# Block one's input projection: the high weights multiply both parts of a row in one 512-column product

## The chip, the cores and the metric

The kernel runs on one core of a Trainium2 chip. The metric is the device time of one execution in microseconds (us). Three executions of the kernel before took 2816.5, 2816.7 and 2818.31 us; the median is 2816.7 us.

## The reference

Two networks of two layers each run one after the other on 256 tokens with 1024 channels, all in float32. The change lies in the first, and in it only in the input projection `h @ w_in`:

```python
for layer in range(DEPTH):                      # DEPTH = 2
    h = _rmsnorm(x, norm1_g[layer])             # x: 256 x 1024
    proj = h @ w_in[layer]                      # 1024 x 3100
    (aq, af, ai, ag, bq, bkc, ..., cq, ck, cv, cf) = jnp.split(proj, split_at, axis=-1)
    o_a = _hgrn2(aq, af, ai, ag, ...)           # gated recurrence, chunks of 64
    o_b = _nsa(bq, bkc, ...)                    # attention over blocks
    o_c = _fox(cq, ck, cv, cf, ...)             # attention with decay
    x = x + concatenate([o_a, o_b, o_c]) @ w_o[layer]
    h2 = _rmsnorm(x, norm2_g[layer])
    x = x + square(relu(h2 @ w_up[layer])) @ w_down[layer]
```

## The kernel before, in words

Nearly all products are made in float32 accuracy out of three passes in the type float32r. A weight tile is split in a high part `w_hi` (ScalarE copies it into float32r, line 776) and a low part `w_lo` (VectorE subtracts, line 800, into the same ring slot). The other operand, a row of 128 channels by 256 tokens, is split likewise into `hn_hi` and `hn_lo`. A product is then low weights times high row (line 839), high weights times high row (line 843) and high weights times low row (line 846), all accumulated in one PSUM bank; the helper is `split_product`.

**The stage in question.** Each layer of the first network begins with the product `in_t`: 18 column tiles of `w_in`, numbered m = 0 to 17 here, each over 8 tiles k of 128 channels. Its result is channel-major: 128 output channels on the partitions, 256 tokens along the free dimension. TensorE runs 24 matmuls of 256 columns for one m, in `block1_pe`. First come 8 of line 839, then 8 pairs of lines 843 and 846; for m = 0 alone the three passes alternate k by k, as the rows of the operand arrive. The results go by turns to PSUM banks 0 and 2, columns 0 to 255. `wait_banks` lets TensorE start m only when the result of m - 2 has been taken out of its bank (semaphore `drained`), and `wait_split` only when `w_lo` of m is there.

**VectorE's queue.** `block1_dve` writes the order by hand. For each m VectorE does, in this order: the pieces of the gated recurrence that are due there (`hg_dve`, lines 1354 to 1427), the low part of the weights of m + 2 (line 800), the scaling of m's result by the row factor `rstd` into `proj` (`input_scaled`, line 1895, which sets `drained`), and, for m = 6 to 13, one scaled row for a later product (line 1885). The recurrence takes its steps by turns of the engines: VectorE writes exponents (lines 1394 and 1398), ScalarE takes their exponential (line 1467), VectorE multiplies (lines 1414 and 1415), TensorE makes 16 small matmuls (line 1329) behind m = 7, 8, 10, 12, 14 and 16, and VectorE takes the scores from PSUM (line 1427). `dve.drain()` makes VectorE wait until what it has issued is written.

**Loads.** A ring of four slots holds the weight tiles. SyncE loads a slot again (line 2946) as soon as the product that used it has ended, ScalarE splits it (line 776), VectorE subtracts (line 800).

**After the stage** comes `in_a`: the first of its products (line 1600, 32 matmuls in the chain's rows) goes to the bank of m = 16 and waits for its `drained`. GpSimd builds blocks from the results 14 and 15 (line 2114).

Of the kernel before, what the change touches and what calls it, by code (L numbers as in the profile page):

```python
# [22 lines left out]
F32R = mybir.dt.float32r  # L23
BF16 = mybir.dt.bfloat16
ALU = mybir.AluOpType
ACT = mybir.ActivationFunctionType
AX_X = mybir.AxisListType.X

P = 128
D = 1024  # L30
KT = D // P
T = 256
# [134 lines left out]
def period(chunks):  # L167

    return next(n for n in range(2, 2 * SLOTS + 1, 2) if n * chunks % SLOTS == 0)
# [399 lines left out]
def kernel_program(nc, streams, consts, params, x_cm, ctx_cm, out_cm, blocks=(1, 2)):  # L569
    with ExitStack() as stack:  # L570
        free = [-(-nc.sbuf_base // 32) * 32]

        def sb(name, shape, dt=F32):

            at = free[0]
            free[0] += -(-4 * int(np.prod(shape[1:])) // 32) * 32
            assert free[0] <= nc.sbuf_usable_end, name
            return nc.alloc_sbuf_tensor_at(name, shape, dt, offset=at)

        def sem(name):  # L580
            return stack.enter_context(nc.semaphore(name))
# [6 lines left out]
        w_lo = [nc.alloc_sbuf_tensor_at(f"w_lo{n}", [P, SLOT_TILES * P], F32R, offset=ring_at + 4 * SLOT_TILES * P * n)  # L588
                for n in range(SLOTS)]
        w_hi = sb("w_hi", [P, SLOTS, SLOT_TILES * P], F32R)  # L590
        res = sb("res", [P, KT, 2 * T])
        hn_hi = sb("hn_hi", [P, KT, 2 * T], F32R)
        hn_lo = sb("hn_lo", [P, KT, 2 * T], F32R)
        hid = sb("hid", [P, FF2 * 2 * T])
        hid_at = free[0] - 4 * FF2 * 2 * T
        work_at = free[0]
# [23 lines left out]
        bank = [stack.enter_context(nc.psum_tensor(f"bank{b}", [P, 512], F32)) for b in range(8)]  # L620
# [36 lines left out]
        proj = proj_b.rearrange("p (m t) -> p m t", t=T)  # L657
# [56 lines left out]
        used = [sem(f"used{s}") for s in range(SLOTS)]  # L714
        drained = [sem(f"drained{p}") for p in range(2)]
        s = Semaphores(sem)
# [37 lines left out]
        def slot_of(lin, g, c):  # L754
            return (lin.chunk + g.at * lin.cpg + c) % SLOTS
# [9 lines left out]
        def split_number(lin, g, j):  # L765

            return lin.split0 + g.at * len(lin.split) + j + g.i * (g.per * len(lin.split))
# [58 lines left out]
        def wait_split(pe, lin, g, c):  # L826
            pe.wait_ge(s.w_lo, split_number(lin, g, lin.split.index(c)) + 1)

        def split_product(pe, lin, g, c, dst, wait_part, x_hi, x_lo, start=True, stop=True, order=None, by_row=False):

            wait_split(pe, lin, g, c)
            slot = slot_of(lin, g, c)
            order = order or range(lin.tiles[c])
            def low_pass(k):
                if g.at == 0:
                    wait_part(0, k)
                pe.matmul(dst, w_lo[slot][:, k * P:(k + 1) * P], x_hi(k), start=(start and k == order[0]), stop=False)  # L839

            def high_passes(k):
                high = w_hi[:, slot, k * P:(k + 1) * P]
                pe.matmul(dst, high, x_hi(k), start=False, stop=False)  # L843
                if g.at == 0:
                    wait_part(1, k)
                return pe.matmul(dst, high, x_lo(k), start=False, stop=(stop and k == order[-1]))  # L846

            if by_row and g.at == 0:
                for k in order:
                    low_pass(k)  # L850
                    mm = high_passes(k)
            else:
                for k in order:
                    low_pass(k)
                for k in order:
                    mm = high_passes(k)
            mm.then_inc(used[slot_of(lin, g, c)], 1)

        def normed_hi(w):
            return lambda k: hn_hi[:, k, 0:w]  # L860

        def normed_lo(w):
            return lambda k: hn_lo[:, k, 0:w]

        def parity(lin, g):
            return (lin.group + g.at) % 2

        def wait_banks(pe, lin, g):

            before = (lin.group + g.at) // 2 + g.i * (g.per // 2)  # L870
            if not (isinstance(before, int) and before == 0):
                pe.wait_ge(drained[parity(lin, g)], before)

        def wait_products(eng, lin, g):

            c = lin.own - 1
            eng.wait_ge(used[slot_of(lin, g, c)], turn_of(lin, g, c) + 1)
# [128 lines left out]
        def streams_before(n):  # L1006
            return sum(norm_width(i) // T for i in range(n))
# [477 lines left out]
        def input_product(pe, lin, g, c, dst, norm, w):  # L1485

            def wait_part(part, k):
                if c == 0:
                    pe.wait_ge((s.norm_hi, s.split_normed)[part], KT * norm + k + 1)

            split_product(pe, lin, g, c, dst, wait_part, normed_hi(w), normed_lo(w))
# [83 lines left out]
        def block1_pe(pe, l):  # L1575
            if l == 0:
                norm_pe(pe, 0)
            lin = PLAN["in_t", l]
            for m in range(lin.n):
                g = Group(m, m, 0, period(1))  # L1580
                wait_banks(pe, lin, g)
                split_product(pe, lin, g, 0, bank[2 * parity(lin, g)][:, 0:T],
                              lambda part, k: pe.wait_ge((s.norm_hi, s.split_normed)[part], KT * 2 * l + k + 1),
                              normed_hi(T), normed_lo(T), by_row=True)
                if m == 0 and l:
                    norm_pe(pe, 2 * l)
                if m == SLOT_DIAG and l == 0:
                    pe.wait_ge(s.consts1, 16)
                hg_pe(pe, l, m)
            lin = PLAN["in_a", l]  # L1590
            for m in range(lin.n):
                g = Group(m, m, 0, period(2))
# [4 lines left out]
                for tt in range(TT):  # L1597
                    q = slice(tt * P, (tt + 1) * P)
                    for k in range(KT):
                        mm = pe.matmul(bank[2 * parity(lin, g)][:, q], sq[:, k, q],  # L1600
                                       ring[slot_of(lin, g, 0)][:, k * P:(k + 1) * P],
                                       start=(k == 0), stop=(k == KT - 1))
                mm.then_inc(used[slot_of(lin, g, 0)], 1)
                compress_pe(pe, l, m, lin, g, 1)
                for u in HEAD_SQUARES[m]:
                    if u == 0:
                        pe.wait_ge(s.hn_sq, l + 1)
                    if u >= 2:
                        pe.wait_ge(s.hn_ln, 5 * l + u - 1)
                    pe.matmul(bank[4 + u % 2][:, :], blk64, sq_b[:, u * 2 * T:(u + 1) * 2 * T],  # L1610
                              start=True, stop=True).then_inc(s.hn_ms, 1)
                if m == 5:
                    pe.wait_ge(s.qkn, l + 1)
                    for u in range(2):
                        pe.matmul(bank[4 + u][:, :], rot, qkn_b[:, (2 + 2 * u) * T:(4 + 2 * u) * T],
                                  start=True, stop=True).then_inc(s.rotated, 1)
# [38 lines left out]
            lin = PLAN["wo", l]  # L1655
            for m in range(lin.n):
                g = Group(m, m, 0, period(1))
# [5 lines left out]
            lin = PLAN["down", l]  # L1663
            for g in turns(pe, lin):
                wait_banks(pe, lin, g)
                for c in range(lin.cpg):
# [3 lines left out]
                                  start=(c == 0), stop=(c == lin.cpg - 1))  # L1670
# [217 lines left out]
        def input_scaled(dve, l, m):  # L1888

            lin = PLAN["in_t", l]  # L1890
            g = Group(m, m, 0, period(1))
            if m == 0:
                dve.wait_ge(s.rstd, streams_before(2 * l) + 1)
            wait_products(dve, lin, g)
            dve.tensor_tensor(proj[:, m, :], bank[2 * parity(lin, g)][:, 0:T], rstd[:, 0:T],
                              ALU.mult).then_inc(drained[parity(lin, g)], 1)

        def square(dve, k, c0, c1):

# [1163 lines left out]
```

## Time and profile before

| | |
|---|---|
| median of three executions | 2816.7 us |
| the profiled execution's own time | 2819.7 us |
| its span in the profile | 2817.5 us |
| TensorE matmuls busy | 2736.7 us (97%), 16508 instructions |
| VectorE busy | 1790.5 us (64%), 3059 instructions |
| ScalarE busy | 1056.1 us (37%) |
| GpSimd busy | 192.0 us (7%) |

The span reaches from the first to the last instruction of the profiled execution; the time of an execution includes a little around it, here 2.2 us. Busy time of an engine is the time covered by its instructions. Matmuls overlap in the pipeline, so the pace of TensorE is read from the distance between starts and not from the duration of one.

### The profile page before, as it was taken

The numbers are of one execution on the slowest core, as the hardware profiler recorded it, in microseconds if no ns is written. First come the engines' busy times: TensorE is split into PE (matmuls) and PEld (weight loads), VectorE is DVE, ScalarE is ACT, GpSimd is POOL, SyncE is SP. The second block draws the span as 40 slices with busy tenths as digits, with TensorE's granted clock in tenths as the row PEclk, the third lists the DMA queues.
The fourth block names the chain that finished last, engine by engine and source line by source line (L and its number), as shares of the span: only waits on it lengthen the run. The fifth ranks groups of instructions, "written<-read, shape, count | busy, mean of one in ns | idle before, by whom it ended". The sixth has DMA issues, their size and how long they took to land.

```text
span 2817.5 us, 45112 instructions
## 1 busy us (share of the span) xinstructions
PE 2736.7 (97%) x16508; PEld 2331.2 (83%) x16508; DVE 1790.5 (64%) x3059; ACT 1056.1 (37%) x1667; POOL 192.0 (7%) x184
## 2 busy tenths in 40 slices
PE   8999999999999999999999999999999999899998
PEld 8669999589988888775777788888788888689998
DVE  8466666566675655597675665655765557757665
ACT  4355443456342221335344322222322213554443
POOL 1000000000000000032213000000000000134000
PEclk9999999999999999999999999999999999999999
DMA  5535554545534443322432244443344433244554
GB/s 202 207 110 193 180 182 159 197 147 184 180 135 149 141 140 132 109 71 70 138 127 67 90 142 149 141 142 127 135 141 147 139 127 125 79 128 158 170 178 157
DMA packets 118649, 401.16 MB, mean 142 GB/s; under 512 B 12928, under 2 KB 20992, under 8 KB 118144
## 3 DMA queue, kind: packets, MB, share of 16 engines
q1 hardware_dynamic: 115408, 392.48, 41.3%
q10 hardware_dynamic: 3120, 7.07, 0.7%
q8 instruction: 76, 1.25, 0.2%
q14 instruction: 45, 0.37, 0.0%
HBM read 398.45 MB, written 1.05 MB: 142 GB/s over the span
## 4 chain that ended last, share of the span: by engine, by line
PE 86%; DVE 5%; issue 4%; DMA 1%; ACT 1%; POOL 1%; DVEq 1%; ACTq 0%; POOLq 0%; SPq 0%
PE bank L839 24%; PE bank L846 24%; PE bank L843 24%; PE bank L1600 2%; DMA ring<-weights 1%; PE bank L2146 1%; PE bank L2505 1%; PE bank L2502 1%; PE bank L2499 1%; DVE work L2267 1%; DVE hn_lo L1072 1%; PE bank L937 1%; POOL w_lo L800 1%; PE bank L1329 1%; PE bank L2175 1%
## 5 line engine op out<-in xcount | busy, mean ns | idle before, releaser
L776 ACT ACTIVATE w_hi<-ring 128x1024 fp32r<-128x1024 f32 (+1 forms) x548 | 572.6, 1046 | 1192.3 <-DMA ring<-weights 1192.2
L800 DVE TENSOR_TENSOR w_lo<-ring,w_hi 128x1024 fp32r<-128x1024 f32 (+1 forms) x538 | 658.7, 1225 | 532.2 <-ACT w_hi L776 528.1
L843 PE MATMUL bank<-hn_hi,w_hi 128*128 128x256 f32 (+1 forms) x2880 | 905.4, 333 | 0.0
L846 PE MATMUL bank<-hn_lo,w_hi 128*128 128x256 f32 (+1 forms) x2880 | 905.1, 333 | 0.0
L843 PEld LDWEIGHTS bank<-hn_hi,w_hi 128*128 128x128 f32 x2880 | 548.5, 190 | 52.2
L846 PEld LDWEIGHTS bank<-hn_lo,w_hi 128*128 128x128 f32 x2880 | 548.5, 190 | 52.2
L839 PE MATMUL bank<-hn_hi,w_lo 128*128 128x256 f32 (+1 forms) x2880 | 577.3, 336 | 11.2 <-DVE w_lo L800 7.7
L839 PEld LDWEIGHTS bank<-hn_hi,w_lo 128*128 128x128 f32 x2880 | 458.4, 190 | 72.5 <-issue 11.1
L843 PE MATMUL bank<-hid_hi,w_hi 128*128 128x512 f32 (+1 forms) x704 | 248.7, 362 | 0.0
L846 PE MATMUL bank<-hid_lo_a,w_hi 128*128 128x512 f32 (+1 forms) x640 | 226.2, 362 | 0.0
L967 DVE SCALAR_TENSOR_TENSOR conds<-ring,con 128x1024 f32<-128x1024 f32 x106 | 130.9, 1235 | 48.3 <-DMA ring<-weights 31.1
L839 PE MATMUL bank<-hid_hi,w_lo 128*128 128x512 f32 (+1 forms) x704 | 156.4, 362 | 0.0
L843 PEld LDWEIGHTS bank<-hid_hi,w_hi 128*128 128x128 f32 x704 | 132.9, 189 | 20.6
L839 PEld LDWEIGHTS bank<-hid_hi,w_lo 128*128 128x128 f32 x704 | 121.9, 189 | 20.6
L846 PEld LDWEIGHTS bank<-hid_lo_a,w_hi 128*128 128x128 f32 x640 | 120.8, 189 | 18.7
L969 DVE SCALAR_TENSOR_TENSOR ring<-ring,con 128x1024 f32<-128x1024 f32 x106 | 131.6, 1241 | 0.0
L843 PE MATMUL bank<-up_hi,w_hi 128*128 128x256 f32 x512 | 125.6, 283 | 0.0
L846 PE MATMUL bank<-up_lo,w_hi 128*128 128x256 f32 x512 | 125.6, 283 | 0.0
L2855 DVE SCALAR_TENSOR_TENSOR hid<-work,par,hid 128x512 f32<-128x512 f32 (+1 forms) x180 | 117.4, 707 | 4.8
L2919 POOL MEMSET work<- 128x1716 f32 x2 | 3.1, 1527 | 1492.0 <-issue 789.3
L843 PEld LDWEIGHTS bank<-up_hi,w_hi 128*128 128x128 f32 x512 | 98.3, 192 | 0.0
L846 PEld LDWEIGHTS bank<-up_lo,w_hi 128*128 128x128 f32 x512 | 98.3, 192 | 0.0
(350 smaller groups left out, 3086.8 us busy)
## 6 DMA issues: line engine op xcount, KB each, us to landing
ring<-weights SPq DMA_DIRECT2D x694, 512.0 KB, 3.4
ring<-weights SPq DMA_DIRECT2D x32, 384.0 KB, 3.1
ring<-weights SPq DMA_DIRECT2D x32, 256.0 KB, 2.9
ring<-weights SPq DMA_DIRECT2D x28, 192.0 KB, 2.4
con<-consts ACTq DMA_DIRECT2D x1, 2063.0 KB, 9.6
con<-consts ACTq DMA_DIRECT2D x1, 1088.0 KB, 5.7
res<-ctx_cm ACTq DMA_DIRECT2D x1, 1024.0 KB, 7.9
con<-params ACTq DMA_DIRECT2D x1, 1024.0 KB, 10.4
```

The source lines that it names most:

```text
L776: act.activation(w_hi[:, slot, 0:w], ring[slot][:, 0:w], ACT.Copy).then_inc(s.w_hi, 1)
L800: eng.tensor_tensor(w_lo[slot][:, 0:w], ring[slot][:, 0:w], w_hi[:, slot, 0:w].bitcast(F32), ALU.subtract).then_inc(s.w_lo, 1)
L839: pe.matmul(dst, w_lo[slot][:, k * P:(k + 1) * P], x_hi(k), start=(start and k == order[0]), stop=False)
L843: pe.matmul(dst, high, x_hi(k), start=False, stop=False)
L846: return pe.matmul(dst, high, x_lo(k), start=False, stop=(stop and k == order[-1]))
L937: mm = pe.matmul(ada_bank(h)[rows, :], cs[:, k, COND_AT - 2 * q:COND_W - 2 * q], ring[slot][:, i * 4 * P:(i + 1) * 4 * P], start=(q == 0 a ...
L967: dve.scalar_tensor_tensor(out=conds[:, :], in0=ring[slot][:, :], scalar=1.0, in1=crow[:, 0:D], op0=ALU.mult, op1=ALU.mult, accum_out=to[: ...
L969: dve.scalar_tensor_tensor(out=ring[slot][:, :], in0=ring[slot][:, :], scalar=1.0, in1=crow[:, D:2 * D], op0=ALU.mult, op1=ALU.mult, accum ...
L1072: last = dve.scalar_tensor_tensor(out=hn_lo[:, k, t], in0=sq[:, k, t], scalar=modulation(l)[:, SHIFT[which], k, c:c + 1], in1=hn_hi[:, k, ...
L1329: mm = pe.matmul(bank[6 + hh][:, c0:c0 + P], keys, queries, start=True, stop=True)
L1600: mm = pe.matmul(bank[2 * parity(lin, g)][:, q], sq[:, k, q], ring[slot_of(lin, g, 0)][:, k * P:(k + 1) * P], start=(k == 0), stop=(k == K ...
L2855: last = dve.scalar_tensor_tensor(out=dst, in0=src, scalar=taps[:, m, k:k + 1], in1=dst, op0=ALU.mult, op1=ALU.add)
```

## The change

The product of the high weights with the high and with the low part of a row becomes one matmul of 512 columns: both parts stand in one tensor, `hn_both`, and the bank's two halves of 256 columns take one result each. The pass of the low weights adds into the first half. VectorE adds the halves with a reduction over the pair, waits for it with a drain, and scales in a second instruction. Both layers are changed (18 results each), and nothing else: other products use `hn_hi` and `hn_lo` as before, at the same addresses. A result takes 8 matmuls of 256 and 8 of 512 columns in place of 24 of 256.

```diff
-        hn_hi = sb("hn_hi", [P, KT, 2 * T], F32R)
-        hn_lo = sb("hn_lo", [P, KT, 2 * T], F32R)
+        hn_both = sb("hn_both", [P, 2, KT, 2 * T], F32R)
+        hn_hi, hn_lo = hn_both[:, 0, :, :], hn_both[:, 1, :, :]
...
+        def joined_product(pe, lin, g, c, wait_part, x_hi, x_both, start=True, stop=True, half=0):
+
+            wait_split(pe, lin, g, c)
+            slot, to = slot_of(lin, g, c), bank[2 * parity(lin, g) + half]
+            rows = lin.tiles[c]
+
+            def low_pass(k):
+                if g.at == 0:
+                    wait_part(0, k)
+                return pe.matmul(to[:, 0:T], w_lo[slot][:, k * P:(k + 1) * P], x_hi(k), start=False, stop=False)
+
+            def high_pass(k):
+                if g.at == 0:
+                    wait_part(1, k)
+                return pe.matmul(to.rearrange("p (u t) -> p u t", u=2), w_hi[:, slot, k * P:(k + 1) * P], x_both(k),
+                                 start=(start and k == 0), stop=(stop and k == rows - 1))
+
+            high_pass(0)
...
+                for k in range(rows):
+                    low_pass(k)
+                for k in range(1, rows):
+                    mm = high_pass(k)
+            mm.then_inc(used[slot], 1)
...
-            dve.tensor_tensor(proj[:, m, :], bank[2 * parity(lin, g)][:, 0:T], rstd[:, 0:T],
-                              ALU.mult).then_inc(drained[parity(lin, g)], 1)
+            dve.tensor_reduce(proj[:, m, :], bank[2 * parity(lin, g)].rearrange("p (u t) -> p t u", u=2), AX_X,
+                              ALU.add)
+            dve.drain()
+            dve.tensor_tensor(proj[:, m, :], proj[:, m, :], rstd[:, 0:T], ALU.mult).then_inc(drained[parity(lin, g)], 1)
```

TensorE's queue at layer 0, m = 8, with the last matmul of m = 7 and the recurrence's 16 small matmuls (one row for 8 of each bank, line 1329 before, 1359 now) ahead of it. Before, where the 8 pairs of lines 843 and 846 follow:

```order
L846 MATMUL bank<-hn_lo,w_hi 128x256
L1329 MATMUL bank<-hid,work 128x128 x8
L839 MATMUL bank<-hn_hi,w_lo_53 128x256 x8
L843 MATMUL bank<-hn_hi,w_hi 128x256
L846 MATMUL bank<-hn_lo,w_hi 128x256
```

And now (line 873 is the matmul of 512 columns, line 868 the pass of the low weights):

```order
L873 MATMUL bank<-hn_both,w_hi 128x512 x7
L1359 MATMUL bank<-hid,work 128x128 x8
L873 MATMUL bank<-hn_both,w_hi 128x512
L868 MATMUL bank<-hn_both,w_lo_53 128x256 x8
L873 MATMUL bank<-hn_both,w_hi 128x512 x7
```

One matmul of the high weights now stands ahead of the low pass, because it opens the whole bank; the other seven stand behind it.

VectorE's queue at layer 0, m = 8 (`hid` holds `proj`, `work` holds `rstd`). Before:

```order
L1394 TENSOR_TENSOR work<-work 128x16x16
L1398 TENSOR_TENSOR work<-work 128x16x16
L1427 COPY_PREDICATED hid<-con_72,bank 128x512 x2
L800 TENSOR_TENSOR w_lo_55<-ring_51,w_hi 128x1024
L1895 TENSOR_TENSOR hid<-bank,work 128x256
L1885 SCALAR_TENSOR_TENSOR work<-res,par_74,work 128x256
```

And now:

```order
L1424 TENSOR_TENSOR work<-work 128x16x16
L1428 TENSOR_TENSOR work<-work 128x16x16
L1457 COPY_PREDICATED hid<-con_71,bank 128x512 x2
L800 TENSOR_TENSOR w_lo_55<-ring_51,w_hi 128x1024
L1925 TENSOR_REDUCE hid<-bank 128x256
L1928 TENSOR_TENSOR hid<-hid,work 128x256
L1915 SCALAR_TENSOR_TENSOR work<-res,par_73,work 128x256
```

No instruction of VectorE changes its place; one is replaced by two.

## Rows read from the trace of the kernel before

**Rows 1.** The page: busy time by engine, chain that ended last by engine.

```profile
PE 2736.7 (97%) x16508; PEld 2331.2 (83%) x16508; DVE 1790.5 (64%) x3059; ACT 1056.1 (37%) x1667; POOL 192.0 (7%) x184
...
PE 86%; DVE 5%; issue 4%; DMA 1%; ACT 1%; POOL 1%; DVEq 1%; ACTq 0%; POOLq 0%; SPq 0%
```

**Rows 2.** Busy time of the engines in the stage, layers 0 and 1.

```profile
core 0: us, PE busy (x) PEld busy (x) DVE busy (x) ACT busy (x) POOL busy (x), PEclk, DMA share, GB/s
...
28.90:74.30 45.40, 45.31 (x409) 43.79 (x410) 41.47 (x73) 18.04 (x20) 6.16 (x8) 1.00 0.46 150
...
415.00:462.50 47.50, 47.50 (x430) 45.98 (x429) 43.14 (x74) 21.07 (x22) 6.18 (x8) 1.00 0.47 156
```

**Rows 3.** Chain of waits (start us, us, what): two passes of 256, two of 512 columns.

```profile
32.12 0.96 PE bank L839 x8
...
35.00 0.96 PE bank L839 x8
...
818.31 1.81 PE bank L839 x8
...
823.75 1.81 PE bank L839 x8
```

**Rows 4.** The same chain where TensorE starts m = 5 of layer 0.

```profile
28.60 0.34 DVE hid L1895
...
28.99 1.21 PE bank L839 x8
```

**Rows 5.** Timeline, VectorE, layer 0 (start us, us, what, [idle before <-releaser]).

```profile
21.88 1.22 DVE L800 TENSOR_TENSOR w_lo<-ring,w_hi 128x1024 fp32r<-128x1024 f32 x1 [2.03 <-ACT w_hi L776]
...
24.45 0.41 DVE L1359 TENSOR_SCALAR work<-work,small 128x256 f32<-128x256 f32 x1 [0.66 <-ACT work L1459]
...
28.52 0.42 DVE L1895 TENSOR_TENSOR hid<-bank,work 128x256 f32<-128x256 f32 x1
28.85 1.22 DVE L800 TENSOR_TENSOR w_lo<-ring,w_hi 128x1024 fp32r<-128x1024 f32 x1
...
50.29 0.42 DVE L1414 TENSOR_TENSOR work<-work 128x256 f32<-128x256 f32 x1 [0.33 <-PE bank L1329]
...
55.60 1.23 DVE L800 TENSOR_TENSOR w_lo<-ring,w_hi 128x1024 fp32r<-128x1024 f32 x1 [0.61 <-ACT w_hi L776]
...
64.37 0.43 DVE L1414 TENSOR_TENSOR work<-work 128x256 f32<-128x256 f32 x1 [0.72 <-PE bank L1329]
...
70.25 0.41 DVE L1895 TENSOR_TENSOR hid<-bank,work 128x256 f32<-128x256 f32 x1
...
81.63 0.42 DVE L1414 TENSOR_TENSOR work<-work 128x256 f32<-128x256 f32 x1 [6.09 <-PE bank L1329]
```

**Rows 6.** Timeline, TensorE: `in_a` starts, layers 0 and 1.

```profile
74.20 1.06 PE L1600 MATMUL bank<-ring,work 128*128 128x128 f32 x8
...
462.53 3.74 PE L1600 MATMUL bank<-ring,work 128*128 128x128 f32 x32
```

**Rows 7.** Timeline, VectorE, layer 1.

```profile
402.35 0.42 DVE L1926 TENSOR_TENSOR work<-bank,work 128x256 f32<-128x256 f32 x1 [2.43 <-PE bank L846]
402.86 0.42 DVE L1929 TENSOR_TENSOR res<-work,res 128x256 f32<-128x256 f32 x1
...
408.03 1.23 DVE L800 TENSOR_TENSOR w_lo<-ring,w_hi 128x1024 fp32r<-128x1024 f32 x1 [0.52 <-ACT w_hi L776]
...
411.85 0.42 DVE L1895 TENSOR_TENSOR hid<-bank,work 128x256 f32<-128x256 f32 x1 [0.84 <-PE bank L846]
...
458.58 0.41 DVE L1895 TENSOR_TENSOR hid<-bank,work 128x256 f32<-128x256 f32 x1
```

**Rows 8.** Groups by form: reductions of VectorE.

```profile
L2184 DVE TENSOR_REDUCE small<-bank 128x1 f32<-128x512 f32 x32 | 22.0, 686 | 8.5 <-PE bank L2146 8.3
...
L1204 DVE TENSOR_REDUCE small<-bank 128x1 f32<-128x256 f32 x40 | 15.1, 419 | 11.3 <-PE bank L1134 10.9
```

More of the change, by code:

```diff
@@ L857, in split_product @@
             mm.then_inc(used[slot_of(lin, g, c)], 1)
+        def joined_product(pe, lin, g, c, wait_part, x_hi, x_both, start=True, stop=True, half=0):
[12 more added lines that the diff above has]
+            high_pass(0)
+            if g.at == 0:
+                low_pass(0)
+                for k in range(1, rows):
+                    low_pass(k)
+                    mm = high_pass(k)
+            else:
+                for k in range(rows):
+                    low_pass(k)
+                for k in range(1, rows):
+                    mm = high_pass(k)
+            mm.then_inc(used[slot], 1)
         def normed_hi(w):
@@ L1581, in block1_pe @@
                 wait_banks(pe, lin, g)
-                split_product(pe, lin, g, 0, bank[2 * parity(lin, g)][:, 0:T],
-                              lambda part, k: pe.wait_ge((s.norm_hi, s.split_normed)[part], KT * 2 * l + k + 1),
-                              normed_hi(T), normed_lo(T), by_row=True)
+                joined_product(pe, lin, g, 0,
+                               lambda part, k: pe.wait_ge((s.norm_hi, s.split_normed)[part], KT * 2 * l + k + 1),
+                               lambda k: hn_hi[:, k, 0:T], lambda k: hn_both[:, :, k, 0:T])
                 if m == 0 and l:
```

## The prediction

> **What bounds the kernel now.** I read the page first. TensorE is busy for 97% of the span and makes 86% of the chain that ended last [rows 1]: fewer TensorE cycles count, if nothing else takes their place. VectorE's 64% is an average over stages. So next I cut out the two stretches in which the changed product runs. There TensorE is busy throughout, but VectorE is busy for 41.47 of 45.40 us in layer 0 and 43.14 of 47.50 us in layer 1, 91% in both, at a TensorE clock of 1.00, its upper level of 2.4 GHz [rows 2]. It has some 4 us to spare per layer, and the change gives it more work there 18 times. Last I looked at who waits for whom. The chain already goes through VectorE once: TensorE starts m = 5 at 28.99, right behind the scaling of m = 3 that ends at 28.94 [rows 4, 5].
>
> **TensorE's part.** Two starts of the 256-column pass lie 35.00 - 32.12 = 2.88 us apart with 24 matmuls between them, 120 ns each; in a 512-column stage it is 823.75 - 818.31 = 5.44 us for 24, 226.7 ns each [rows 3]. One 512-column matmul in place of two of 256 saves 240 - 226.7 = 13.3 ns. There are 8 x 18 x 2 = 288 such pairs, 3.8 us in all, or 0.107 us for each m (2.77 in place of 2.88 us). That is the whole gain, since the array still streams the same columns; 288 weight loads go too, but the gap between starts already contains what they cost. The Trainium skill (TensorE: Matmul & The Clock Gate, "Back-to-back issue gap") gives a fixed 2.5 ns per warm matmul on top of N/2.4; by it the gaps would be 109.2 and 215.8 ns and the whole gain 0.7 us. The rows show about 13 ns above the streaming time at both widths, so I go by them.
>
> No row has a moving operand made of two pieces. Below, that costs nothing; above, I estimate the point at which it would matter. From 50.29 to 64.37 VectorE handles four m's, with 0.61 and 0.72 us idle [rows 5], so two take it (14.08 - 1.33) / 2 = 6.4 us now and 7.9 us after the change. TensorE has two m's and 16 small matmuls to do in that time, now 14.08 / 2 = 7.04 us and then 6.83. Sixteen wide matmuls could each be 65 ns slower before it showed. I cost it at nothing.
>
> **VectorE's part.** One scaling of 0.42 us becomes a reduction, a drain and a scaling. The nearest row for the reduction is one of 512 PSUM elements at 686 ns [rows 8]. A drain between two dependent instructions sets the second 0.51 us behind the first where the first lasts 0.42 (lines 1926 and 1929) [rows 7]: 0.09 us. The second instruction is a 256-element product, 0.42 us like the one removed, and what follows can start 0.33 us behind its start as now (28.52 to 28.85) [rows 5]. So each m adds **a = 0.69 + 0.09 = 0.78 us** to VectorE's queue. The bounds of the reduction: 0.42 us if it went by its 256 outputs, as a reduction of 256 elements does [rows 8], so a = 0.51; twice 0.686 us if the stride of 256 between the two addends halved its rate, so a = 1.46. I take 0.69, the row with the same number of elements read from PSUM. The Trainium skill (VectorE: DVE Perf Modes, the section on the TRN2 errata) has a cycle table, 120 + N from PSUM and 58 + N within SBUF at 0.96 GHz. It would make a 0.66 + 0.09 + 0.33 - 0.39 = 0.68 and the total below 9.0 instead of 11.9 us. The traced 0.42 and 0.69 us are longer than its values, and the sum uses them.
>
> **What reaches the end.** Behind the reduction stand, on VectorE's queue, the scaling that frees the bank for m + 2, the low weights of m + 3 and every piece of the recurrence; TensorE waits for each of them. I follow the queue to the scaling of m = 16, for which `in_a` must wait.
>
> Layer 0. The reductions of m = 0 and 1 are covered, because VectorE idles 2.03 us for ScalarE at 21.88 [rows 5]. Of m = 2's 0.78 us the idle 0.66 before line 1359 covers all but 0.12 [rows 5]. From m = 3 on the queue is nearly full: the idle pieces are 0.33, 0.61 and 0.72 us, 1.66 in all [rows 5]. VectorE now finishes the scaling of m = 16 at 70.66; it would finish 0.12 + 14 x 0.78 - 1.66 = 9.38 us later, at 80.04, and `in_a` would start at 80.09 in place of 74.20 [rows 6]: **+5.9 us**. TensorE's own end gives less: m = 17 needs the bank of m = 15, ready at 68.38 + 0.12 + 13 x 0.78 - 1.66 = 76.98, and ends 2.77 later, at 79.8.
>
> Layer 1. The reductions of m = 0 and 1 are covered by the idle 0.52, 0.19 and 0.84 us ahead of m = 2 (two of them in [rows 7]). From m = 2 on there are 15 reductions up to m = 16, and idle pieces of 0.17, 0.57, 0.33, 0.35 and 0.75 us, 2.17 in all. The scaling of m = 16, now ending at 458.99, would end 11.70 - 2.17 = 9.53 us later, at 468.52, and `in_a` start at 468.57 in place of 462.53: **+6.0 us**.
>
> TensorE's 3.8 us are hidden: it arrives early and waits for VectorE. The sum is +11.9 us. Against the profiled execution's 2819.7 us that is 2831.6; the median of the runs lies 3.0 us lower, so I forecast 2816.7 + 11.9 = **2828.6 us**. Behind the stage I expect no recovery: the ring is only four slots deep, so the weight loads start later by as much, and VectorE idles 6.09 us at its next wait [rows 5], so it no longer matters there. Late next in the stage are the low weights and, once, the recurrence: its matmuls behind m = 8 wait for scores that VectorE takes at about 45.6 in place of 41.7.
>
> **The rivals.**
>
> *The reduction is dearer (0.10).* Its two addends stand 1 KB apart, and no row has such a read. At twice the price each of the 29 uncovered reductions adds another 0.69 us: 19.9 us more, 2848.5 us. For it: it is unmeasured. Against it: element for element, VectorE's PSUM reads of 512 elements all take about 0.69 us in this trace.
>
> *The reduction is cheaper (0.08).* At a = 0.51 the sum falls by 29 x 0.27 = 7.8 us: 2820.8 us, not distinguishable from before.
>
> *VectorE's slack covers it (0.05).* The place is the scaling of m = 16. `in_a` starts on time in layer 0 if 14a is at most 74.20 - 0.05 - 70.66 - 0.12 + 1.66 = 5.03 us, and in layer 1 if 15a is at most 462.53 - 0.05 - 458.99 + 2.17 = 5.66 us: a up to 0.36 us. Then TensorE's gain shows, for 13 m's in layer 0 (the wait at m = 5 eats the first five) and 18 in layer 1: 31 x 0.107 = 3.3 us, 2813.4 us. Against it: even the lower bound of a is 0.51. By the fixed gap of the Trainium skill's page TensorE: Matmul & The Clock Gate this would be 2816.1 us.
>
> *Half is caught up later (0.07).* Behind the stage TensorE also has idle time; if part of it depends on something that does not move, each layer gives back about 3 us: 2822.6 us. Against it: every load and every engine there follows TensorE's own progress.
>
> **How the numbers follow.** My forecast has 0.70. About 0.2%, 5.6 us, is what a measurement of this kernel can tell from no change: faster is below 2811.1, slower above 2822.3. Slower: the forecast, the dear reduction and half of the recovery, 0.70 + 0.10 + 0.04 = 0.84. The same: the cheap reduction, the covered case and the other half, less a small part, 0.14. Faster: 0.02. For the range, a between 0.65 and 0.95 alone gives 2824.8 to 2833.5; I reach down to 2820.5, which takes in the cheap reduction and the recovery, and up to 2840, a reduction half as dear again (10 us more), which leaves out the doubled one.
>
> **What would show it.** In the profile after: reductions of about 0.69 us, 36 of them, and the multiply 0.78 us behind each; 512-column starts 227 ns apart; VectorE without gaps from m = 3 to m = 16; TensorE idle in the stage, with the scaling, the low weights or the recurrence's scores as releaser; `in_a` starting near 80.1; the distance from there to layer 1's stage unchanged. The forecast is wrong if TensorE shows no new idle time there, or if the reduction lasts over 0.95 us.

## The result and the profile after

| | before | after |
|---|---|---|
| median of six executions each | 2816.6 us | 2831.1 us |
| lowest to highest | 2815.68 to 2818.86 | 2827.9 to 2831.58 |
| span of the profiled execution | 2817.5 us | 2829.7 us |
| its own time | 2819.7 us | 2831.5 us |

The ratio is 1.0047, with a 95% interval of 1.0037 to 1.0057: 13.2 us slower, 10.4 to 16.1. The two medians lie 14.5 us apart. The forecast was 2828.6 us, 11.9 us slower. Among the experiments below, three executions (one of e3, two of e10) took between 5354 and 11227 us; they are in no median here.

The page of the kernel after begins with these rows, which answer to [rows 1]:

```profile
PE 2742.1 (97%) x16220; PEld 2320.4 (82%) x16220; DVE 1812.5 (64%) x3095; ACT 1052.9 (37%) x1667; POOL 196.2 (7%) x184
...
PE 84%; DVE 6%; issue 4%; DMA 2%; DVEq 1%; ACT 1%; POOL 1%; ACTq 0%; SPq 0%; POOLq 0%
```

TensorE has 288 matmuls fewer, but busy time on the page says little. The busy time in the stage of the two layers, against [rows 2] (the window and its length, then TensorE, weight loads, VectorE, ScalarE, GpSimd, the granted clock, DMA share, GB/s), tells more; the third row is a short piece that is discussed at the end:

```profile
28.80:79.50 50.70, 46.62 (x305) 38.46 (x305) 48.77 (x82) 16.25 (x19) 7.13 (x8) 0.97 0.40 135
418.90:472.50 53.60, 48.84 (x317) 40.04 (x315) 51.52 (x87) 19.31 (x22) 7.13 (x8) 0.97 0.42 138
46.00:50.50 4.50, 4.50 (x18) 3.90 (x18) 4.17 (x9) 1.06 (x1) 0.00 (x0) 0.62 0.02 4
```

VectorE is now busy for 96% of the stage in both layers (91% before), and TensorE for 92 and 91% (over 99% before). The two have changed roles. TensorE's timeline in layer 0 (start us, duration us, what, idle before and its releaser) shows where it waits:

```profile
28.84 0.50 PE L873 MATMUL bank<-hn_both,w_hi 128*128 128x512 f32 x1 [1.10 <-DVE hid L1928]
...
35.71 0.50 PE L873 MATMUL bank<-hn_both,w_hi 128*128 128x512 f32 x1 [1.02 <-DVE hid L1928]
...
44.68 1.16 PE L1359 MATMUL bank<-work 64*128 64x128 f32 x16 [1.82 <-DVE hid L1457]
...
75.98 0.50 PE L873 MATMUL bank<-hn_both,w_hi 128*128 128x512 f32 x1 [0.61 <-DVE hid L1928]
...
79.48 2.72 PE L1630 MATMUL bank<-ring,work 128*128 128x128 f32 x22 [0.44 <-DVE hid L1928]
```

The releaser is VectorE each time: the scaling (line 1928) or, once, the recurrence's scores (line 1457). `in_a` starts at 79.48 in place of 74.20 [rows 6]. VectorE's timeline, for m = 3 and 4 and at the end of the stage:

```profile
27.60 0.69 DVE L1925 TENSOR_REDUCE hid<-bank 128x256 f32<-128x512 f32 x1
28.36 0.43 DVE L1928 TENSOR_TENSOR hid<-hid,work 128x256 f32<-128x256 f32 x1
28.70 1.22 DVE L800 TENSOR_TENSOR w_lo<-ring,w_hi 128x1024 fp32r<-128x1024 f32 x1
29.84 0.68 DVE L1925 TENSOR_REDUCE hid<-bank 128x256 f32<-128x512 f32 x1
...
50.42 0.69 DVE L1925 TENSOR_REDUCE hid<-bank 128x256 f32<-128x512 f32 x1 [0.26 <-PE bank L873]
...
76.01 0.99 DVE L1424 TENSOR_TENSOR work<-work 128x256 f32<-128x256 f32 x1
76.93 0.94 DVE L1428 TENSOR_TENSOR work<-work 128x256 f32<-128x256 f32 x1
77.80 0.68 DVE L1925 TENSOR_REDUCE hid<-bank 128x256 f32<-128x512 f32 x1
78.55 0.88 DVE L1928 TENSOR_TENSOR hid<-hid,work 128x256 f32<-128x256 f32 x1
```

The reduction takes 0.68 to 0.69 us and the scaling starts 0.76 us behind it. What follows starts 28.70 - 27.60 = 1.10 us behind the reduction, where it started 0.33 us behind the single scaling [rows 5]: a result adds 0.77 us to VectorE's queue. The idle 0.26 us at 50.42 is the only gap that the timeline shows in it from m = 3 to m = 16.

In both layers the comparison below uses three numbers of each profile: the start of `in_a` in layer 0, the length of layer 1's stage (from the first matmul of its norm, 405.03 before, to the start of `in_a`), and the median of the whole. Changes are against the profile of before (74.20 and 57.50 us).

| kernel | `in_a`, layer 0 | stage, layer 1 | sum | median | ratio, 95% interval |
|---|---|---|---|---|---|
| after | +5.28 | +6.06 | +11.3 | 2831.1 | 1.0047 [1.0037, 1.0057] |
| e6, after unaltered | +5.66 | +6.11 | +11.8 | 2833.45 | 1.0055 [1.0041, 1.0069] |
| e1, no reduction | -1.15 | -1.20 | -2.3 | 2816.02 | 0.9997 [0.9988, 1.0006] |
| e2, narrow matmuls | +5.20 | +5.70 | +10.9 | 2828.26 | 1.0048 [1.0035, 1.0061] |
| e3, ScalarE copies half | +3.71 | +3.68 | +7.4 | 2826.98 | 1.0034 [1.0022, 1.0046] |
| e4, reduction alone | +0.59 | -0.33 | +0.3 | 2819.01 | 1.0006 [0.9997, 1.0015] |
| e5, reduction twice | +14.61 | +15.84 | +30.5 | 2848.57 | 1.0113 [1.0098, 1.0129] |
| e7, layer 1 alone | +0.23 | +6.13 | +6.4 | 2823.86 | 1.0027 [1.0017, 1.0036] |
| e8, GpSimd later | +4.08 | +4.84 | +8.9 | 2829.62 | 1.0049 [1.0035, 1.0062] |
| e9, e3 and e8 and an order | +2.41 | +2.53 | +4.9 | 2827.84 | 1.0035 [1.0021, 1.0049] |
| e10, before unaltered | -0.25 | +0.48 | +0.2 | 2818.77 | 1.0003 [0.9993, 1.0013] |

The kernel before, run beside them, had medians of 2816.64 (e1 to e4), 2816.52 (e5 to e8) and 2816.48 us (e9, e10).

### The profile page after: what moved, and what is told of

Same layout as the page of the kernel before. It is cut to its first block, busy times and chain, and to the rows that moved or that the text cites. A ratio compares the mean times of both kernels' runs of the same rounds, so it can differ in the third digit from the quotient of the medians.

```text
span 2829.7 us, 44608 instructions
## 1 busy us (share of the span) xinstructions
PE 2742.1 (97%) x16220; PEld 2320.4 (82%) x16220; DVE 1812.5 (64%) x3095; ACT 1052.9 (37%) x1667; POOL 196.2 (7%) x184
## 4 chain that ended last, share of the span: by engine, by line
PE 84%; DVE 6%; issue 4%; DMA 2%; DVEq 1%; ACT 1%; POOL 1%; ACTq 0%; SPq 0%; POOLq 0%
PE bank L839 23%; PE bank L846 23%; PE bank L843 23%; PE bank L1630 2%; DMA ring<-weights 2%; DVE w_lo L800 1%; PE bank L2178 1%; PE bank L2537 1%; PE bank L2534 1%; PE bank L2531 1%; PE bank L967 1%; POOL w_lo L800 1%; DVEq L1927 1%; PE bank L1539 1%; PE bank L2207 1%
## 5 line engine op out<-in xcount | busy, mean ns | idle before, releaser
L843 PE MATMUL bank<-hn_both,w_hi 128*128 128x256 f32 (+1 forms) x2592 | 834.2, 338 | 0.0
L846 PE MATMUL bank<-hn_both,w_hi 128*128 128x256 f32 (+1 forms) x2592 | 834.0, 338 | 0.0
L839 PE MATMUL bank<-hn_both,w_lo 128*128 128x256 f32 (+1 forms) x2592 | 533.0, 341 | 9.7 <-DVE w_lo L800 8.0
L843 PEld LDWEIGHTS bank<-hn_both,w_hi 128*128 128x128 f32 x2592 | 493.3, 190 | 52.1
L846 PEld LDWEIGHTS bank<-hn_both,w_hi 128*128 128x128 f32 x2592 | 493.2, 190 | 52.0
L839 PEld LDWEIGHTS bank<-hn_both,w_lo 128*128 128x128 f32 x2592 | 420.8, 190 | 68.6 <-issue 10.4
```

## The experiments

The expectations call the theories T1 (VectorE's added time sets the stage and hides what TensorE gains), T2 (the 512-column matmul or TensorE's clock is what got slower) and T3 (joining saves only 2.5 ns a pair).

**e1: the joined product alone.** VectorE works as before, and the second half of the bank is never added.

```diff
-            dve.tensor_reduce(proj[:, m, :], bank[...].rearrange("p (u t) -> p t u", u=2), AX_X, ALU.add)
-            dve.drain()
-            dve.tensor_tensor(proj[:, m, :], proj[:, m, :], rstd[:, 0:T], ALU.mult).then_inc(...)
+            dve.tensor_tensor(proj[:, m, :], bank[2 * parity(lin, g)][:, 0:T], rstd[:, 0:T],
+                              ALU.mult).then_inc(drained[parity(lin, g)], 1)
```

> The changed kernel, in which VectorE does what it did before: one multiply of 256 elements, from the bank's first half (the product of the low part of the row is computed but left out of the sum, in both layers). Theory 1 (the cost is VectorE's added time a per result, 0.77 us, and TensorE's gain is hidden behind it): with a = 0 the gain shows, 31 results x 0.107 us = 3.3 us, so 2813.3 us; in_a of layer 0 starts near 72.8 and of layer 1 about 3 us earlier than before; no wait for line 1928's place of over 2 us. Theory 2 (the 512-column product itself is slower, by its operand in two pieces or by TensorE's lower clock): 2820 us or more, since nothing of it is undone here. Theory 3 (the two weight loads and matmuls saved are worth only about 2.5 ns a pair): 2816.1 us.

Measured: `in_a` starts 1.15 us earlier in layer 0, and layer 1's stage is 1.20 us shorter. The whole slowdown is gone with VectorE's part of it. In layer 0 TensorE waits once, 1.69 us ahead of m = 5 as before, and from there on never again; in layer 1 it never waits. Its clock is 1.00 (windows view of e1, columns as above):

```profile
28.60:73.00 44.40, 44.25 (x304) 37.48 (x305) 41.65 (x73) 18.29 (x20) 6.15 (x8) 1.00 0.46 152
414.40:458.60 44.20, 44.11 (x306) 37.30 (x305) 40.82 (x72) 18.84 (x21) 6.16 (x8) 1.00 0.48 155
```

T2 falls: the wide matmul is no slower. T3's 0.2 to 0.3 us per layer is too little, but my 1.4 and 1.9 us were too much, 2.35 in place of 3.3 us in all. Nor is all of the 2.35 TensorE's gain. m = 5 starts 0.28 us earlier than before (28.71 against 28.99), because the split by ScalarE that VectorE waits for ahead of m = 2 [rows 5] starts 0.29 us earlier (20.50 against 20.79), and that start varies by itself: it is 20.53 in e10, the kernel before once more. From the start of m = 5 to `in_a` it is 44.34 us against 45.21, so 13 results gain 0.87 us there. That and the 1.20 us of layer 1 make some 0.07 us for each result. In the time of an execution even this doesn't show: 0.9997, with 1 in the interval.

**e2: VectorE's part alone, nearly.** Six of the eight wide matmuls of a result are two of 256 columns again, into the same two halves; m = 0 keeps all eight wide.

```diff
-                for k in range(1, rows):
-                    mm = high_pass(k)
+                for k in range(1, rows - 1):
+                    high = w_hi[:, slot, k * P:(k + 1) * P]
+                    pe.matmul(to[:, 0:T], high, x_hi(k), start=False, stop=False)
+                    pe.matmul(to[:, T:2 * T], high, x_both(k)[:, 1, :], start=False, stop=False)
+                mm = high_pass(rows - 1)
```

> VectorE as in the changed kernel (reduction, drain, multiply), TensorE nearly as before: of each result's 8 products of 512 columns, six are split again into two of 256 (the first and the last stay wide, m = 0 keeps all), same sums. Theory 1: TensorE's pace of 2.85 us is still faster than VectorE's, so the time is that of the changed kernel, 2831 us, within 1.5 us; in_a starts at 79.5 in layer 0. Theory 2: back towards 2817 to 2820 us. Theory 3 says the same as theory 1.

Measured: a ratio of 1.0048 against 1.0047, and stages within 0.1 and 0.4 us of those of after. Whether TensorE has its gain or not makes no difference once VectorE adds the halves. This and e1 are the two halves of T1.

**e3: less work for VectorE.** ScalarE copies the upper half out of PSUM; VectorE adds it with an instruction of 256 elements in place of 512.

```diff
+                act.activation(rope_t[:, m % 2 * T:(m % 2 + 1) * T], bank[2 * parity(lin, g)][:, T:2 * T],
+                               ACT.Copy).then_inc(s.upper, 1)
...
-            dve.tensor_reduce(proj[:, m, :], bank[...].rearrange("p (u t) -> p t u", u=2), AX_X, ALU.add)
+            dve.wait_ge(s.upper, lin.n * l + m + 1)
+            dve.tensor_tensor(proj[:, m, :], bank[...][:, 0:T], rope_t[:, m % 2 * T:(m % 2 + 1) * T], ALU.add)
```

> The changed kernel with a cheaper add: ScalarE copies the bank's upper half into SBUF (about 0.4 us, on an engine with 27 us to spare per layer), VectorE adds it to the lower half with a product-sized instruction of 0.42 us instead of the 0.69 us reduction, drain and multiply as now; the sum is the same. Theory 1: a falls from 0.77 to 0.51, 29 x 0.26 = 7.5 us less than the changed kernel: 2823.5 us; up to 2826 if ScalarE's splits, now queued behind its copy, come late. Theory 2: 2831 us.

Measured: 3.71 and 3.68 us in the stages, less than after but more than expected; 2826.98 us in place of 2823.5, and above the 2826 that were allowed for late splits. VectorE's queue in e3 has two new waits for ScalarE's copy, at m = 2 and at m = 16:

```profile
24.61 0.42 DVE L1933 TENSOR_TENSOR hid<-bank,work 128x256 f32<-128x256 f32 x1 [1.69 <-ACT work L1810]
...
74.96 0.94 DVE L1429 TENSOR_TENSOR work<-work 128x256 f32<-128x256 f32 x1
76.94 0.42 DVE L1933 TENSOR_TENSOR hid<-bank,work 128x256 f32<-128x256 f32 x1 [1.04 <-ACT work L1810]
```

ScalarE's own queue explains both. The copy of m = 2 stands behind a split, a table load and three activations of the recurrence; the copy of m = 16 stands behind the exponential that needs VectorE's exponents.

```profile
21.68 1.28 ACT L1488 ACT_TABLE_LOAD   x1
...
24.14 0.37 ACT L1810 ACTIVATE work<-bank 128x256 f32<-128x256 f32 x1
...
75.93 0.63 ACT L1498 ACTIVATE work<-work 128x512 f32<-128x512 f32 x1 [5.48 <-DVE work L1429]
76.47 0.36 ACT L1810 ACTIVATE work<-bank 128x256 f32<-128x256 f32 x1
```

TensorE had finished m = 16 at about 72.8, so the copy could have run in ScalarE's idle 5.48 us; instead VectorE waited for it afterwards, 1.04 us. The first wait makes TensorE wait 1.78 us for the scaling of m = 3, until 30.43, where it went on at 28.84 in after. Layer 1 has the same two waits, 1.76 and 1.04 us (before 416.59 and 468.56). The direction agrees with T1; the expected size left these waits out.

**e4: a smaller a, 0.27 us.** The reduction stays and drain and scaling go, so the row factor is left out of the results.

```diff
             dve.tensor_reduce(proj[:, m, :], bank[...].rearrange("p (u t) -> p t u", u=2), AX_X,
-                              ALU.add)
-            dve.drain()
-            dve.tensor_tensor(proj[:, m, :], proj[:, m, :], rstd[:, 0:T], ALU.mult).then_inc(...)
+                              ALU.add).then_inc(drained[parity(lin, g)], 1)
```

> The changed kernel with the reduction alone: the row factor is left out (drain and multiply gone), so a = 0.69 - 0.42 = 0.27 us per result, below the 0.36 us that VectorE's slack was worked out to cover. Theory 1: TensorE is the bound again, its gain shows, 2813 to 2815 us, and in_a of layer 0 starts between 72.8 and 74. If the slack is really smaller, with the same mechanism, up to 2818. Theory 2: 2825 us or more.

Measured: +0.59 us in layer 0 and -0.33 us in layer 1, where e1 has -1.15 and -1.20; 2819.01 us, which is above the expected 2813 to 2815 and the 2818 allowed beyond it. I had put the point from which the slack covers a at 0.36 us, so 0.27 should have been free. TensorE's timeline of e4 shows why it wasn't:

```profile
29.39 0.50 PE L873 MATMUL bank<-hn_both,w_hi 128*128 128x512 f32 x1 [2.15 <-DVE hid L1925]
...
33.47 2.29 PE L873 MATMUL bank<-hn_both,w_hi 128*128 128x512 f32 x8
...
43.24 1.16 PE L1359 MATMUL bank<-work 64*128 64x128 f32 x16 [0.83 <-DVE hid L1457]
```

The first wait is the one of 1.7 us at m = 5 that both before and e1 have, grown by half a microsecond. In the second row eight wide matmuls last 2.29 us, where they last 2.00 elsewhere: the eighth belongs to m = 7 and starts some 0.3 us late, behind the reduction of m = 5 that ends at 35.20. The third wait is new, the scores behind m = 8. Past it TensorE never waits again in this stage. Against e1, m = 5 starts 0.68 us later, m = 7 0.95 us and the scores 1.74 us, and `in_a` the same 1.74 us. Of the first 0.68 us only about 0.26 is the longer reduction; the other 0.42 is ScalarE's split, which starts at 20.92 here and at 20.50 in e1, the start that varies by itself. Layer 1 has no such first wait and loses 0.87 us, 0.15 at m = 7 and 0.72 at the scores. So the end of the stage had the slack that I computed, but TensorE had already lost time at earlier points, and a TensorE that works without a pause does not make it up.

**e5: a larger a.** A second reduction of the same bank, into a scratch tile.

```diff
+            dve.tensor_reduce(rope_t[:, 0:T], bank[2 * parity(lin, g)].rearrange("p (u t) -> p t u", u=2), AX_X,
+                              ALU.add)
```

> The changed kernel with a second, useless reduction per result (into scratch, ahead of the real one, not drained between): 0.60 us more of VectorE per result. Theory 1 (a queue of VectorE without gaps sets the stage): 14 results in layer 0 and 15 in layer 1 each pass it on in full, so in_a starts 8.4 us later than in the changed kernel in layer 0 (87.9) and the stage of layer 1 is 9.0 us longer; 17.4 us in all, about 2848 us. If something else than VectorE's queue set part of the stage (ScalarE's splits, the loads, TensorE's clock), less than 12 us.

Measured: the stages are 9.33 and 9.78 us longer than those of after, the execution 2848.57 us. The second reduction starts 0.60 us behind the first, with no drain between them (VectorE's timeline of e5):

```profile
37.43 0.69 DVE L1925 TENSOR_REDUCE work<-bank 128x256 f32<-128x512 f32 x1
38.03 0.68 DVE L1927 TENSOR_REDUCE hid<-bank 128x256 f32<-128x512 f32 x1
38.79 0.43 DVE L1930 TENSOR_TENSOR hid<-hid,work 128x256 f32<-128x256 f32 x1
```

I had expected 8.4 and 9.0 us, for 14 and 15 results. But the change had already used up the idle time that had covered the first ones: the scaling of m = 3 ends at 31.16 us in e5 and at 28.79 in after, 2.37 us later, which is four reductions. All 17 from m = 0 to m = 16 at 0.60 us would be 10.2 us; 0.72 of that is offset, since the gap of 0.26 us at 50.42 is gone and the last scaling lasts 0.42 us in place of 0.88. Once VectorE's queue is full, each added microsecond is paid in full; this is the straight part of the line whose foot e4 found.

**e6: the kernel after, unaltered,** for how well a kernel repeats.

> The changed kernel once more, unaltered, for a second profile and a narrower interval. The stages should repeat within 0.3 us (in_a at 79.5 in layer 0, a stage of 63.5 us in layer 1). Theory 1: what the whole time shows beyond the 11.4 us of the stages differs from execution to execution outside them, so the rest of the span need not be longer than before. Rival: the changed program is really 2 us longer outside the stages as well, and then both profiles show it.

Measured: stages of +5.66 and +6.11 us against +5.28 and +6.06, ratio 1.0055, its interval overlapping that of the first measurement. In a stage the profile repeats within 0.4 us, a total within 2.4 us.

**e7: the change in layer 1 alone.** Layer 0 uses `split_product` and the single scaling.

```diff
+                if l == 0:
+                    split_product(pe, lin, g, 0, bank[2 * parity(lin, g)][:, 0:T],
...
+            if l == 0:
+                dve.tensor_tensor(proj[:, m, :], bank[2 * parity(lin, g)][:, 0:T], rstd[:, 0:T],
+                                  ALU.mult).then_inc(drained[parity(lin, g)], 1)
+                return
```

> The change in layer 1 only; layer 0 as before. Theory 1: in_a of layer 0 starts at 74.2 as before, the stage of layer 1 takes 63.5 us in place of 57.5, and the time is 6.0 us above before, 2822.7 us. If the two layers' costs were shared (one hides the other), less than 4 us or over 8 us.

Measured: layer 0 as before within 0.23 us, layer 1 +6.13, the total +7.3 us. The layers add up and don't act on each other, and the total shows nothing given back behind the stage.

**e8: GpSimd's blocks after the last scaling.** Three products and one scaling near the end of the stage last 0.88 to 0.99 us in place of 0.42 while GpSimd builds its blocks. Here GpSimd waits for result 16.

```diff
+                wait_drained(pool, PLAN["in_t", l], 16)
```

> The changed kernel with one wait added on GpSimd: its blocks (line 2146 there, 3.1 us twice a layer) start only after the result of m = 16 is scaled. In the profile of the changed kernel VectorE's products with both inputs in SBUF take 0.95 in place of 0.42 us while GpSimd works (lines 1445, 1424, 1428), and these stand ahead of the scaling of m = 16, for which in_a waits. Theory: these four instructions give back 1.7 us per layer, in_a of layer 0 starts near 77.8 and the stage of layer 1 takes 61.8 us; 3.4 us less than the changed kernel in all, unless TensorE then waits for the blocks. Rival: these instructions are long for another reason, and nothing moves.

Measured: the instructions are short again (VectorE's timeline of e8, the counterpart of the last four rows of after above),

```profile
75.40 0.43 DVE L1424 TENSOR_TENSOR work<-work 128x256 f32<-128x256 f32 x1
75.74 0.42 DVE L1428 TENSOR_TENSOR work<-work 128x256 f32<-128x256 f32 x1
76.08 0.69 DVE L1925 TENSOR_REDUCE hid<-bank 128x256 f32<-128x512 f32 x1
76.84 0.42 DVE L1928 TENSOR_TENSOR hid<-hid,work 128x256 f32<-128x256 f32 x1
```

and the scaling of m = 16 ends at 77.26 in place of 79.43. `in_a` gains only 1.20 and 1.22 us, since TensorE's m = 17 then ends last. The total shows nothing of it (1.0049).

**e9: e3 and e8 together.** e3's copy, e8's wait, and the copy of m = 16 ahead of the exponential.

```diff
-                hg_act(act, l, m)
+                if m != 16:
+                    hg_act(act, l, m)
...
+                if m == 16:
+                    hg_act(act, l, m)
```

> Two remedies together on the changed kernel: the add with ScalarE's copy of the upper half (its copy for m = 16 now ahead of the recurrence's exponential) and GpSimd's blocks only after m = 16. In the profile of the first remedy VectorE stood idle 1.04 us for ScalarE's copy of m = 16 and lost time to GpSimd. Theory 1: in_a of layer 0 starts 1.5 to 2.5 us earlier than with the first remedy alone (77.9), at 75.4 to 76.4, the stage of layer 1 takes 58.7 to 59.7 us, and the time is 3 to 5 us above before, about 2820.5 us. It does not beat the kernel before, since VectorE's scaling of m = 3 and its first scores, early in the stage, still come late. If it does, under 2816 us, the early waits don't matter.

Measured: the stages are the shortest with sum and row factor in place, +2.41 and +2.53 us, as the mechanism says. The wait for the copy of m = 2 is still there, 1.69 us before 24.44 and 1.76 before 418.31, so this is not the best that could be had. But the total is 2827.84 us, no better than e3, where about 2820.5 was expected. The time is outside the stages, and e10 was run beside it to judge that.

**e10: the kernel before, unaltered.**

> The kernel before, unaltered, as a control of the time outside the two stages. From in_a of layer 0 to the norm of layer 1 its one profile has 330.8 us, from in_a of layer 1 to the end 2355.0 us; the two profiles of the changed kernel have 329.5 and 329.2, and 2357.2 and 2359.2 us. Theory: these differences are from execution to execution, and a second profile of before lies anywhere between 2351 and 2359 us in the last part, the stages repeating within 0.3 us (74.2; 57.5 us). Rival: the changed program is some 2 us slower there, and before repeats 2355.0 or less.

Measured: 1.0003, stages -0.25 and +0.48 us, so a stage repeats within 0.5 us and not within 0.3. Of the 0.48 us 0.22 are a wait of TensorE for a scaling in layer 1 (at 415.69) that the first profile does not have. Its median of 2818.77 us is 2.3 us above the shared median of the same kernel, so the median of a single kernel can be off by that much. The expectation's rival was that the changed program is slower outside the stages as well. From `in_a` of layer 1 to the end of the span e10 has 2354.2 us, before 2355.0 and the two profiles of after 2357.2 and 2359.2, which alone would speak for the rival. But e2 has 2351.1 and e8 2354.3 us there with the sum in place in both layers, so the part varies by more than the difference, and no slowness of the changed program is shown. Part of the spread is the granted clock of TensorE. The stretch from the start of `in_a` in layer 0 to layer 1's norm holds the same instructions of TensorE in every kernel. The rows are of e8, of e10 and of e9 (windows view of each, columns as above):

```profile
127.63:141.63 14.00, 12.06 (x77) 4.88 (x77) 10.11 (x38) 3.26 (x13) 0.95 (x1) 1.00 0.87 316
...
78.28:405.70 327.42, 320.85 (x2669) 282.22 (x2668) 201.47 (x438) 163.03 (x319) 6.16 (x8) 1.00 0.53 177
```

```profile
123.30:137.30 14.00, 10.97 (x67) 4.93 (x69) 8.88 (x31) 2.71 (x11) 0.95 (x1) 0.88 0.74 272
73.95:402.90 328.95, 321.39 (x2678) 283.26 (x2677) 198.84 (x434) 162.50 (x318) 0.95 (x1) 0.99 0.52 176
```

```profile
126.00:140.00 14.00, 11.45 (x56) 4.62 (x56) 7.67 (x24) 1.74 (x6) 0.95 (x1) 0.64 0.72 259
```

With a mean clock of 1.00 the whole stretch takes 327.4 us, with 0.99 329.0; e9 (0.98) takes 333.5 us. The difference lies mainly at one place, the 14 us behind a wait of TensorE for VectorE of 2.0 us that all twelve profiles have: there the clock is 1.00 on average in e8, 0.88 in e10 and eight others, before and after among them, and 0.64 in e9 and e4. e4, with nothing in common with e9 at that place, has the same 0.98 and 332.8 us. Over the 53 executions of the kernel before beside e1 to e10, the span is 2817.4 us in the median where the mean clock was 0.989 or 0.990, 2814.2 at 0.992 and 2813.4 at 0.993. e9's five executions had 0.988 to 0.990. By the fit to those 53 (1.2 us for 0.001 of mean clock) that would explain 2.7 of the 6.5 us by which e9's total exceeds its stages. The rest, and the 1 to 5 us by which the other kernels' medians lie above the sum of their stages, e10's included, stays open. No kernel here beats the kernel before in time.

## Why the prediction was right

**The bound.** Right. VectorE took over the stage; e1 and e2 show it from both sides, e5 gives the slope.

**a = 0.78 us.** It is 0.77. The reduction costs by its input: 0.68 to 0.69 us for 512 elements of PSUM, though its two addends lie 1 KB apart. The rivals of a dear and of a cheap reduction are out. The drain gap was 0.08 us in place of 0.09.

**TensorE's gain.** Two starts of the low pass that wait for nothing (19.43 and 22.22 us in TensorE's timeline) lie 2.79 us apart, against 2.88 before and 2.77 predicted. By the fixed 2.5 ns of the Trainium skill (TensorE: Matmul & The Clock Gate, "Back-to-back issue gap"), which the section gives for an isolated matmul, it would be 2.60 us; the trace does not agree, here as in [rows 3]. Nor does a moving operand of two pieces cost much: 0.02 us in a result at most. The term of 0.107 us for a result was too large. Between two results it is 0.09 us; over two results with the recurrence's small matmuls between them it is 0.15 us (from 49.01 to 56.05 before, from 48.38 to 55.27 in e1). e1 shows about 0.07 us for each of its results, in layer 1 without any wait.

**Layer 0, +5.9 us.** It was +5.28. The step that was off is what was covered before m = 3: I had VectorE 0.90 us late there, and it was 0.15 us early (28.79 against 28.94 at the end of the scaling). Two pieces of slack were missing from the sum. The first is an idle 0.49 us of "issue" ahead of line 1366 in layer 0. It stands in the profiles of before, e1, e4, e7 and e10, in whose layer 0 a result takes VectorE one instruction, and in none of the seven where it takes two or more. It is thus a piece that the added work covers, and it was to be seen in the trace of before. What VectorE does in it, no profile shows. The second is chance: ScalarE split the weights that VectorE waited for 0.56 us earlier (20.23 against 20.79), but both kernels' second profiles have the same 20.53 (e6 and e10). Against it stood two things that I had not foreseen: the scaling of m = 16 itself ran into GpSimd's work (0.88 in place of 0.42 us), and the gap of 0.26 us at 50.42.

**Layer 1, +6.0 us.** It was +6.06; the scaling of m = 16 ends 9.55 us later, counted from the norm, and the sum had 9.53. That close a hit is partly luck: the same 0.46 us on the last scaling (471.58 to 472.47) and a gap of 0.25 us at 443.46 were in it too, so some 0.7 us of the added work must have been covered that the sum charged. Where stays open.

**The total.** The median is 2831.1 us, 2.5 above the forecast, while the stages give 11.3 us, 0.6 below it. Of the 14.5 us between the medians 3.2 are not in the stages; e10, with nothing changed, has 2.1 us of that kind.

**The waits.** Right: the scaling, and once the recurrence's scores, foreseen at 45.6 and ending at 44.6 us. "VectorE without gaps from m = 3 to m = 16" was right but for 0.26 us. The distance from `in_a` to layer 1's norm is 329.48 against 330.83 us, within what it varies by in kernels with the same instructions there.

**The rival on the other side.** It was rightly out, since a is over its threshold, but the threshold of 0.36 us was wrong. I looked for the slack at the scaling of m = 16 alone. e4 has 0.27 us and still loses 1.7 us in layer 0, 0.4 of it by chance, and 0.9 in layer 1 against e1: m = 5 in layer 0, m = 7 and above all the scores behind m = 8 bind first. The price of that rival was too good as well, 3.3 us for a gain that e1 measures at 2.35 in the stages, or 2.1 without the early start, and at nothing certain in the total.

**Recovery behind the stage.** None is seen: e7's layer 1 costs 6.13 us and its total 7.3. A single median can be 2.3 us off, so this excludes the 3 us for a layer that the rival wanted, but not much less.

## What to carry to other kernels

Before shifting work from the busiest engine to the second one, read the second engine's share in the stage concerned and not over the kernel: 64% overall was 91% here, and it had room for 0.2 us in a result where the change asked for 0.77. When such slack is computed, compute it at every wait along the stage, because an engine without pauses never makes up what an early wait took. A matmul of twice the columns in place of two saved 0.09 us for eight pairs at best, 11 ns each, and pays only if the addition moved elsewhere is free.

## What the runs showed of the hardware that I had not expected

**TensorE's clock fell behind a short wait.** After the 1.82 us wait for the scores the granted clock went to its lower level of 1.2 GHz: the window from 46.00 to 50.50 above has a mean of 0.62. The matmuls of m = 9 show it in TensorE's timeline of after, the first two rows against the next two:

```profile
46.16 1.91 PE L868 MATMUL bank<-hn_both,w_lo 128*128 128x256 f32 x8
47.87 2.74 PE L873 MATMUL bank<-hn_both,w_hi 128*128 128x512 f32 x8
50.45 1.12 PE L868 MATMUL bank<-hn_both,w_lo 128*128 128x256 f32 x8
51.40 1.77 PE L873 MATMUL bank<-hn_both,w_hi 128*128 128x512 f32 x7
```

It happened in both layers of after, e6 and e8, and the price in the stage was the 0.26 and 0.25 us for which VectorE then waited. But the wait alone does not decide it. e5 waits 3.02 us at this place in layer 0 and 3.01 in layer 1, and the 5 us behind it have the upper level throughout in the one and the lower in the other (windows view of e5, columns as above):

```profile
49.45:54.45 5.00, 5.00 (x40) 4.50 (x41) 4.92 (x10) 1.27 (x2) 0.00 (x0) 1.00 0.00 0
451.69:456.69 5.00, 5.00 (x27) 4.58 (x28) 4.55 (x9) 1.27 (x2) 0.00 (x0) 0.50 0.02 5
```

e2 falls to 0.66 in layer 0 and keeps 1.00 in layer 1, both behind 1.71 us, and its layer 1 is 0.36 us shorter than that of after. e7 keeps 1.00 behind 1.81 us in its changed layer 1; its stage is as long as that of after (+6.13 us), but there VectorE stands idle 0.45 us of "issue" ahead of a scaling (at 463.29) instead. So the lower clock is a quarter of a microsecond of the 6 us that a layer costs. What makes it fall in one case and not in the other stays open.

**GpSimd slows some of VectorE's instructions and not others.** While GpSimd builds its blocks (line 2146, in after from 71.29 and 76.00 us), products of 256 elements with both inputs in SBUF last 0.94 to 0.99 us in place of 0.42, the scaling of m = 16 lasts 0.88, and the reduction from PSUM between them stays at 0.68. e8 moves GpSimd's work and gets 0.42 back. The Trainium skill (SBUF — State Buffer, "Who interferes with whom") says that a VectorE instruction with two SBUF inputs contends with a GpSimd instruction that reads SBUF, and that a reduction never does; the trace agrees. The lengthening goes the other way as well: while VectorE subtracts the weights from 73.52 to 74.82 (line 800, two SBUF inputs, 1.30 us in place of 1.22), GpSimd's instruction that started at 73.69 lasts 1.71 us, where the middle one of the eight lasts 0.79. The scaling that this change puts behind the reduction has two SBUF inputs, where the single one of before had an input in PSUM and kept its 0.41 us at 70.25, in the middle of GpSimd's work from 68.45 to 71.57: moving the factor behind the reduction also exposed it to GpSimd.
